# In which order a mixture-of-experts kernel queues its expert weights

## The reference, cut to what matters

```python
# block 1 (block 2 has the same shape, with w1, w3, w2 and other norms)
for g in range(N_GROUPS):                                    # 4 groups of 8 experts
    a = jnp.einsum('td,edf->tef', t, w_gate[g])              # 1024 -> 256 per expert
    b = jnp.einsum('td,edf->tef', t, w_up[g])
    m = jax.nn.silu(a) * b * combine[:, g, :, None]
    y = y + jnp.einsum('tef,efd->td', m, w_down[g])          # 256 -> 1024
```

## Time and profile before

| What | us |
|---|---|
| three executions | 922.36, 923.57, 924.17 |
| median | 923.57 |
| span of the profiled execution (the page gives it no other time) | 921.0 |
| PE busy | 864.4 (94% of the span) |
| DVE busy | 504.2 (55%) |
| ACT busy | 349.9 (38%) |
| SP's hardware queue, time of its packets | 75.4% of the span of 16 DMA engines |

### The profile page before, as it was taken

The page is one execution under the profiler, slowest core; times in us unless marked ns, Lnnn a source line. Parts: engine busy times, 40 slices in busy tenths (PEclk is TensorE's granted clock), DMA queues, the critical chain, the costliest instruction groups (busy, mean ns, idle before and its releaser), DMA issues.

```text
span 921.0 us, 14919 instructions
## 1 busy us (share of the span) xinstructions
PE 864.4 (94%) x5634; PEld 554.7 (60%) x5634; DVE 504.2 (55%) x1112; ACT 349.9 (38%) x689; POOL 22.3 (2%) x41
## 2 busy tenths in 40 slices
PE   8999999999999998998777899999899999999994
PEld 6778558887976533443333389877565455455552
DVE  5877568455456666333333476888854533333335
ACT  5674435446355322222222457744521111111113
POOL 1010111000000000000000000000000000000000
PEclk9999999999999999999999999999999999999998
DMA  9655891546548999999999996530959899999991
GB/s 354 250 202 222 319 374 51 189 148 253 202 165 316 412 424 403 424 425 423 425 426 424 424 354 241 204 138 1 370 206 418 337 421 428 422 424 425 427 405 49
DMA packets 30242, 288.46 MB, mean 313 GB/s; under 512 B 3144, under 2 KB 5608, under 8 KB 8944
## 3 DMA queue, kind: packets, MB, share of 16 engines
q1 hardware_dynamic: 26688, 281.40, 75.4%
q0 software_dynamic: 1136, 3.74, 1.2%
q10 hardware_dynamic: 2368, 2.64, 0.9%
HBM read 286.70 MB, written 1.06 MB: 312 GB/s over the span
## 4 chain that ended last, share of the span: by engine, by line
PE 65%; DMA 15%; DVE 12%; ACT 4%; issue 3%; SPq 1%; DVEq 0%; ACTq 0%
DMA ring<-in_experts 13%; PE bank L1157 12%; PE bank L1177 8%; PE bank L736 7%; PE bank L738 7%; PE bank L737 7%; PE bank L1205 5%; PE bank L1162 3%; DVE ring_r L526 2%; PE bank L1169 2%; PE bank L1113 2%; DMA ring<-in_ada 1%; PE bank L862 1%; PE bank L1259 1%; DMA ring<-in_lat 1%
## 5 line engine op out<-in xcount | busy, mean ns | idle before, releaser
L526 DVE TENSOR_TENSOR ring_r<-ring,ring_r 128x1024 fp32r<-128x1024 f32 (+1 forms) x84 | 99.4, 1212 | 67.9 <-ACT ring_r L519 67.7
L1157 PE MATMUL bank<-ring,arena 128*64 128x256 f32 x1024 | 117.6, 382 | 0.9 <-DVE arena L2500 0.6
L519 ACT ACTIVATE ring_r<-ring 128x1024 fp32r<-128x1024 f32 (+1 forms) x84 | 84.9, 1045 | 69.6 <-PE bank L738 68.4
L736 PE MATMUL bank<-HT_r,ring_r 128*128 128x256 f32 x352 | 101.7, 289 | 1.5 <-DVE arena_r L2066 0.7
L738 PE MATMUL bank<-HT_r,ring_r 128*128 128x256 f32 x352 | 99.6, 283 | 0.0
L1157 PEld LDWEIGHTS bank<-ring,arena 128*64 128x64 f32 x1024 | 71.6, 137 | 38.0 <-issue 6.4
L1177 PE MATMUL bank<-ring,arena 128*64 128x512 f32 (+1 forms) x496 | 93.7, 604 | 0.7 <-DVE arena L2574 0.7
L1773 ACT ACTIVATE arena<-bank 128x256 f32<-128x256 f32 (+1 forms) x65 | 31.8, 489 | 140.5 <-PE bank L1157 82.4
L737 PE MATMUL bank<-XN_r,ring_r 128*128 128x256 f32 x288 | 81.5, 283 | 0.0
L2547 DVE SCALAR_TENSOR_TENSOR arena<-bank,arena 128x512 f32<-128x512 f32 x33 | 24.8, 750 | 101.8 <-PE bank L1177 101.7
L1162 PE MATMUL bank<-ring,arena 128*32 128x512 f32 x480 | 59.2, 611 | 21.7 <-DMA ring<-in_experts 21.2
(11 more groups left out here) (490 smaller groups left out, 1420.3 us busy)
## 6 DMA issues: line engine op xcount, KB each, us to landing
ring<-in_experts SPq DMA_DIRECT2D x62, 2048.0 KB, 15.6
ring<-in_experts SPq DMA_DIRECT2D x62, 1024.0 KB, 12.8
ring<-in_ada SPq DMA_DIRECT2D x12, 2048.0 KB, 9.2
ring<-in_win SPq DMA_DIRECT2D x5, 2048.0 KB, 13.9
ring<-in_hy SPq DMA_DIRECT2D x3, 2048.0 KB, 18.5
ring<-in_mk SPq DMA_DIRECT2D x2, 2048.0 KB, 13.0
ring<-in_mv SPq DMA_DIRECT2D x2, 2048.0 KB, 9.5
ring<-in_wo SPq DMA_DIRECT2D x2, 2048.0 KB, 8.6
```

Of the source, the lines that this page charges most:

```text
L519: nc.scalar.activation(R(h), w, ACT.Copy).then_inc(sem("w_high"), 1)
L526: nc.vector.tensor_tensor(R(w), w, R(h), ALU.subtract).then_inc(sem("w_low"), 1)
L736: mm(ps, R(ah), R(bh), start=first, stop=False)
L1157: last = mm(gu_bank[g * wide:(g + 1) * wide, 0:256], xw[:, k, :], w[k // 4][:, k % 4, g * 256:(g + 1) * 256], start=k == 0, stop=k == KD - 1)
```

## The change

In both blocks SP issues Ge+1 before De. The waits stay with their DMAs. In the unrolled part the first expert's G now has no D behind it, and each later G is followed by the D of the expert before; in the loop the same holds, with the wait for `down_done` one lower, since it belongs to expert e - 1. The last D, D31, gets its own place: in block 1 right after the loop, in block 2 behind the gate/up weights of the extra window. Neither the bytes nor the number of DMAs changes, nor does anything on the other engines.

```diff
                     sp.wait_ge(sem(f"gu_done{b + 1}"), last_user + 1)
                     sp.dma_start(ring[:, slot(base + q), 0:GU], w[e, :, 0:GU]).then_inc(sem(f"slot_full{slot(base + q)}"), 16)
-                    sp.wait_ge(sem(f"down_done{b + 1}"), last_user + 1)
-                    sp.dma_start(ring[:, slot(base + q), GU:SLOT], w[e, :, GU:SLOT]).then_inc(sem(f"slot_down{q}"), 16)
+                    if e > RING + ways:
+                        q = (e - 1 - ways) % RING
+                        last_user = e - 1 - RING - ways * (e - 1 < 2 * RING + ways)
+                        sp.wait_ge(sem(f"down_done{b + 1}"), last_user + 1)
+                        sp.dma_start(ring[:, slot(base + q), GU:SLOT], w[e - 1, :, GU:SLOT]).then_inc(sem(f"slot_down{q}"), 16)
                 with sp.Fori(first, NE - RING + 1, RING) as e0:
                     for r in range(RING):
...
                         sp.wait_ge(sem(f"gu_done{b + 1}"), e0 + (r - RING + 1))
                         sp.dma_start(ring[:, s, 0:GU], src[:, 0:GU]).then_inc(sem(f"slot_full{s}"), 16)
-                        sp.wait_ge(sem(f"down_done{b + 1}"), e0 + (r - RING + 1))
-                        sp.dma_start(ring[:, s, GU:SLOT], src[:, GU:SLOT]).then_inc(sem(f"slot_down{q}"), 16)
+                        q = (r - 1 - ways) % RING
+                        before = w[bass.ds(e0 + (r - 1), 1)].rearrange("a p f -> p (a f)")
+                        sp.wait_ge(sem(f"down_done{b + 1}"), e0 + (r - RING))
+                        sp.dma_start(ring[:, slot(base + q), GU:SLOT], before[:, GU:SLOT]).then_inc(sem(f"slot_down{q}"), 16)
+
+                def last_down():
+
+                    q = (NE - 1 - ways) % RING
+                    sp.wait_ge(sem(f"down_done{b + 1}"), NE - RING)
+                    sp.dma_start(ring[:, slot(base + q), GU:SLOT], w[NE - 1, :, GU:SLOT]).then_inc(sem(f"slot_down{q}"), 16)
+
+                if b == 0:
+                    last_down()
...
                     sp.wait_ge(sem("gu_done2"), NE - RING + 1)
                     sp.dma_start(ring[:, slot(base + 3), 0:GU], src[:, 0:GU]).then_inc(sem(f"slot_full{slot(base + 3)}"), 16)
+                    last_down()
                     sp.wait_ge(sem("down_done2"), NE - RING + 1)
```

More of the change, by code:

```diff
@@ L639, in experts @@
                     sp.dma_start(ring[:, slot(base + q), 0:GU], w[e, :, 0:GU]).then_inc(sem(f"slot_full{slot(base + q)}"), 16)
-                    sp.wait_ge(sem(f"down_done{b + 1}"), last_user + 1)
-                    sp.dma_start(ring[:, slot(base + q), GU:SLOT], w[e, :, GU:SLOT]).then_inc(sem(f"slot_down{q}"), 16)
+                    if e > RING + ways:
[3 more added lines that the diff above has]
+                        sp.dma_start(ring[:, slot(base + q), GU:SLOT], w[e - 1, :, GU:SLOT]).then_inc(sem(f"slot_down{q}"), 16)
                 with sp.Fori(first, NE - RING + 1, RING) as e0:
                     for r in range(RING):
-                        q = (r - ways) % RING
-                        s = slot(base + q)
+                        s = slot(base + (r - ways) % RING)
                         src = w[bass.ds(e0 + r, 1)].rearrange("a p f -> p (a f)")
```

## The result

The changed kernel takes 924.83 us (median of 19 runs, 923.01 to 927.45) against 922.76 us of the kernel before (19 runs): the ratio is 1.0021, 95% interval 1.0012 to 1.0029. It is slower by about 2 us, just past the 0.2% that I had called the limit of what can be told, and inside the range of the prediction. The forecast was built on 923.57 for the kernel before, which came out 0.8 us lower in these runs; its change of +0.1 us is to be held against the measured +2.1.

A forecast was written before the change was run, and what follows sets the result against it. Block 1's experts were taken as bound by the DMA byte stream, block 2's by PE. From 923.57 us, 0.7 (ada11) and 0.3 (block 2) gained and 1.1 lost to the low clock gave 923.7 us, range 921.6 to 925.0.

The forecast's parts named there:

- Steady order and the end of block 1: Block 1's experts: G lands 2.47 us earlier, steps end 3.7 us earlier; the order alone gains 0 in front of ada11.
- Thin places: Block 1, 353 to 356 and 361 to 364 us: two underfed DMA stretches get filled, 1.2 us gained (bounds 0 and 1.4).
- The load of in_gates_w: End of block 1: released earlier on POOL's queue, it shares the DMA engines with ada11 and costs 0.5 us (bounds 0, 1.2).
- ada11 in all: End of block 1: ada11 lands 0.7 us earlier, 1.2 from filled DMA stretches less 0.5 for sharing.
- The longer wait: PE before ada(11): wait grows from 0.75 to 3.7 us, the clock falls and costs 1.1 us (bounds 0, 1.5).
- the likeliest case: Behind the wait for ada11 the clock falls and the stream's gain is about eaten: 923.7 us, chance 0.55.
- Block 2: Block 2's experts, bound by PE: the stream gets further ahead, but only PE's 0.29 us weight wait goes; gain 0.3 us.
- The sum: Whole kernel: 1.0 us gained, 1.1 given back where the clock falls, from 923.57 to 923.7 us.
- Same: Whole kernel: time within about 0.2%, 1.85 us, of the kernel before; chance 0.78.
- The kept G: Rival: block 1's steps run 2.47 us earlier and nothing takes it back; 919.6 us, chance 0.12.
- The slower rival: End of block 1: thin places stay, in_gates_w costs 1.2 us, the fallen clock 1.5; 926.0 us, chance 0.08.

The follow-up runs named there:

- e4: Changed kernel with the load of in_gates_w held back until the transposes are in; 923.21 us, 0.9998 of the kernel before.
- e11: Kernel before with the load of in_gates_w held back until the transposes are in; 922.53 us, 0.9995 of the kernel before.
- e9: Changed kernel with six filler matmuls before ada(11) and the load of in_gates_w held back; 921.12 us, 0.9983 of the kernel before.
- e3: Changed kernel with eight filler matmuls between the transposes and ada(11); 923.04 us, 0.9997 of the kernel before.
- e1: New issue order in block 1 alone, the old one in block 2; 924.48 us, 1.0014 of the kernel before.
- e2: New issue order in block 2 alone, the old one in block 1; 922.22 us, 0.9993 of the kernel before.
- e12: Changed kernel with ada(11) moved behind the first chunk of the xl projection and four filler matmuls ahead of xl; 920.52 us, 0.9981 of the kernel before.
- e6: Changed kernel with ada(11) moved behind the first chunk of the xl projection; 922.50 us, 0.9998 of the kernel before.
- e5: Kernel before with eight filler matmuls between the transposes and ada(11); 924.63 us, 1.0016 of the kernel before.
- e8: Changed kernel with ada(11) behind the first chunk of xl and the load of in_gates_w held back; 922.27 us, 0.9999 of the kernel before.
- e10: Kernel before with only half of each expert's down weights fetched in block 1's loop, so the output differs; 899.39 us, 0.975 of the kernel before.
- e7: Kernel before with ada(11) moved behind the first chunk of the xl projection; 924.15 us, 1.0017 of the kernel before.

## Why the prediction was right, and where its sizes were off

*Steady order and the end of block 1.* Right. Steps 3.9 us earlier (3.7 said), no wait at L1191 for down weights, and nearly all of it lost in front of ada11. Most of PE's waits for experts stay (17.7 us of 21.2; 3.5 are missing, and the wait for ada11 has grown by 3.8): 

```profile
PE bank L1176 <- DMA ring<-in_experts: 17.7, 12, 2.1
...
PE bank L876 <- DMA ring<-in_ada: 4.6, 1, 4.6
```

*Thin places.* Right, both filled. What they brought shows only with the sharing out of the way: from the load at 288 us to ada(11) it is 531.45 - 288.02 = 243.43 us before, 531.36 - 288.41 = 242.95 after, and 529.85 - 287.94 = 241.91 in e4. The old order without the sharing is e11's 242.85, and the new one without it is 241.91 in e4 and 242.17 in e9: 0.7 to 0.9 us, where 1.2 was taken.

*The load of in_gates_w.* The mechanism was right, and the size nearly so, but by luck. The new order pays 0.8 (e3 against e9) to 1.3 us (e1 against e4), about the full 1.2 of the load's bytes. I had taken 0.5 and forgotten that the old order shares as well; it pays 0.3 to 0.6 (e11), hardly more than executions of one order differ by. The term is the difference of the two, about 0.4 to 0.7 us. "DMA: Bandwidth & Descriptors", section "Issuing engines are not separate DMA queues", of the Trainium skill says that DMAs issued by different engines run on the same 16 DMA engines and interleave, and e4 agrees: with POOL's load held back, ada11 on SP's queue is ready 1.0 to 1.3 us earlier.

*ada11 in all.* 0.7 was said; it is 0.48 earlier in this pair of traces. The same stretch is 243.16 in e2, 243.20 in e1 and 242.98 in e3, so executions of one order differ by up to 0.3 us and the gain is somewhere between 0 and 0.5.

*The longer wait.* This is the term that decided, and the one that was mis-sized. The clock fell, as the likeliest case had it. I took 1.1 us, since part of the slow stretch would lie in the idle time; it was 2.0, above the bound of 1.5. The bound came from one fall of 3.4 us. Here the low clock held for twice as long: the windows after have 0.73, 0.50, 0.50 and 0.56 in a row, which is from about 528.9 to 535.7. 2.5 us of it lay in the idle time, and 4.3 us over PE's work. "TensorE: Matmul & The Clock Gate", section "Loop structure matters more than you think", warned of the low clock behind a wait for data; the trace agrees with 3.64 us for 1.92.

*Block 2.* Right: 0.36 gained, 0.3 said, no wait for weights, and its experts stay at the upper level. (Near 650 us, in its mixer, the clock falls in the changed kernel as in the one before.)

*The sum* was -0.7 - 0.3 + 1.1 = +0.1. With the measured sizes it is -0.5 - 0.36 + 2.0 = +1.2 in the trace, and +2.1 in the medians. Part of the rest is the offset of 0.39 in this execution; I have no experiment for what is left, and both lie within the spread of single executions. That 924.83 lies inside the range is in part luck: the forecast's base was 0.8 us too high, and 923.57 + 2.1 would have been 925.7, above its 925.0. "Same" had the highest chance and the middle of the measurement is at its edge; "slower" had 0.08, and the result stands where it begins, by a larger clock term and a smaller gain at ada11 alone.

*The rivals.* The kept G (919.6) fell with ada11's wait. The slower rival had the right place and took the sharing at its full 1.2 us and the clock at 1.5; the clock cost even more. But it had the thin places stay, and they were filled.

## What to carry to other kernels

When a queue is full, a new order in it moves only who waits, and the gain goes to the first consumer that stands behind the same bytes: look for that one before counting. Time won ahead of such a wait is idle time, and idle time of TensorE can cost more than it was; give it work (fillers brought 2.2 us in e3 against the change and 1.6 in e12 against e6) or don't make it. Fillers longer than the wait cost time: in e5, without a wait to cover, 1.5 us. When loads move earlier, look at which other queue's loads are released with them.

## What the runs showed of the hardware

The length of a single wait doesn't tell whether the clock falls. Behind a wait of 2.26 us for expert weights e6 stayed at the upper level, and e12 behind 2.08 us, while e8 fell behind 2.07 us; e6 gives:

```profile
502.34 1.92 PE L1176 MATMUL bank<-ring,arena 128*32 128x512 f32 x16 [2.26 <-DMA ring<-in_experts]
```

and e8:

```profile
509.74 3.27 PE L1176 MATMUL bank<-ring,arena 128*32 128x512 f32 x16 [2.07 <-DMA ring<-in_experts]
```

The same wait can go either way. At 351 us PE waits 2.00 to 2.02 us for VectorE in all of these kernels, in the old order and in the new (e10 aside). In the executions of the changed kernel, e1, e2, e6, e9, e11 and e12 the clock fell to 0.72 or 0.73 over 351 to 357; in those of the kernel before, e3, e4, e5, e7 and e8 it stayed at 1.00. The row behind the wait, in the changed kernel and in e3:

```profile
351.14 1.85 PE L1219 MATMUL bank<-arena_r 64*128 64x512 f32 x8 [2.01 <-DVE arena_r L2568]
```

```profile
350.64 1.20 PE L1219 MATMUL bank<-arena_r 64*128 64x512 f32 x8 [2.01 <-DVE arena_r L2569]
```

In block 1 such a fall cost nothing: from the load at 288 us to ada(11) it is 242.95 us in the changed kernel and 242.98 in e3. In the mixer of block 2 it does. From ada(11)'s columns to block 2's experts the work is the same in all of them. It took 131.7 to 131.8 us where the clock fell once, near 650 us, as in the kernel before and the changed one (behind a wait of 1.86 us); 131.2 to 131.3 in e2, e4, e7 and e12, where it didn't fall; and 133.3 and 133.4 in e5 and e11, where it fell near 612 too. That is 0.5 and 1.6 us of difference from one execution to the next, which may be a good part of the 3 to 4 us over which the runs of one kernel spread; only one execution of each kernel was traced, so this share isn't shown.
